# Two weight-row pairs of each gate/up column block as seven products of block sums

## The reference, cut to what matters

```python
D_FF = ((8 * D_MODEL + 3 * 256 - 1) // (3 * 256)) * 256     # 5632
h = _rmsnorm(x, ffn_norm[l])
gate, up = jnp.split(h @ w_gate_up[l], 2, axis=-1)
x = x + (jax.nn.silu(gate) * up) @ w_down[l]
```

## Time and profile before

| what | value |
|---|---|
| median of 3 runs | 2871.65 us (2871.58 to 2873.06) |
| span of the profiled execution | 2869.4 us |
| TensorE busy | 2863.4 us |
| VectorE busy | 1852.1 us |
| ScalarE busy | 1339.4 us |
| GpSimd busy | 868.4 us |

### The profile page before, as it was taken

How to read it: one execution, slowest core, us unless ns; L and a number is a source line. 1 busy time by engine, 2 the same in 40 slices (tenths; PEclk the granted TensorE clock), 3 DMA queues, 4 the chain that set the end, 5 groups by cost and what they waited for, 6 DMA issues and landing times.

```text
span 2869.4 us, 35463 instructions
## 1 busy us (share of the span) xinstructions
PE 2863.4 (100%) x12860; PEld 2372.1 (83%) x12860; DVE 1852.1 (65%) x2277; ACT 1339.4 (47%) x1564; POOL 868.4 (30%) x1477
## 2 busy tenths in 40 slices
PE   9999999999999999999999999999999999999999
PEld 8888888888888888888888888888888888888887
DVE  7599866687655555545575998666876555555554
ACT  5445554554544444444444455445545444444443
POOL 0055267355222322300000652773452313213000
PEclk9999999999999999999999999999999999999999
DMA  7666666776666666666666666667766666666554
GB/s 247 182 186 199 201 192 194 229 238 194 196 192 192 195 191 193 194 193 194 193 193 177 198 192 197 191 194 233 238 194 196 191 193 193 191 195 191 194 193 170
DMA packets 291296, 567.39 MB, mean 198 GB/s; under 512 B 18984, under 2 KB 24944, under 8 KB 291184
## 3 DMA queue, kind: packets, MB, share of 16 engines
q1 hardware_dynamic: 283888, 540.54, 61.8%
q10 hardware_dynamic: 7296, 25.44, 2.7%
HBM read 551.23 MB, written 14.68 MB: 197 GB/s over the span
## 4 chain that ended last, share of the span: by engine, by line
PE 98%; DVE 1%; ACT 0%; issue 0%; DMA 0%; DVEq 0%; ACTq 0%
PE acc L481 64%; PE acc L486 32%; PE acc L528 1%; DVE w_lo L1193 1%; PE acc L526 1%; PE acc L539 0%; DVE arena L1193 0%; DVE tmp L1193 0%; PE acc L519 0%; ACT w_hi L812 0%; PE acc L540 0%; DMA xs<-in_x_dram 0%; DVE arena L1211 0%; PE acc L498 0%; PE acc L654 0%
## 5 line engine op out<-in xcount | busy, mean ns | idle before, releaser
L1193 DVE TENSOR_TENSOR w_lo<-w_raw,w_hi 128x1024 fp32r<-128x1024 f32 x1024 | 1261.6, 1236 | 970.4 <-ACT w_hi L812 965.8
L812 ACT ACTIVATE w_hi<-w_raw 128x1024 fp32r<-128x1024 f32 x1024 | 1084.0, 1060 | 1461.4 <-PE acc L486 1414.6
L481 PE MATMUL acc<-w_hi,opa_hi 128*128 128x512 f32 (+1 forms) x2364 | 927.8, 392 | 0.6 <-ACT w_hi L812 0.6
L481 PE MATMUL acc<-w_hi,opa_lo 128*128 128x512 f32 (+1 forms) x2364 | 917.6, 388 | 0.0
L481 PE MATMUL acc<-w_hi,opb_hi 128*128 128x512 f32 x1728 | 672.9, 389 | 0.2
L481 PE MATMUL acc<-w_hi,opb_lo 128*128 128x512 f32 x1728 | 672.3, 389 | 0.0
L486 PE MATMUL acc<-w_lo,opa_hi 128*128 128x512 f32 (+1 forms) x2364 | 629.9, 388 | 0.1
L481 PEld LDWEIGHTS acc<-w_hi,opa_hi 128*128 128x128 f32 x2364 | 444.0, 188 | 94.4 <-issue 3.7
L486 PEld LDWEIGHTS acc<-w_lo,opa_hi 128*128 128x128 f32 x2364 | 442.7, 188 | 92.4 <-DVE w_lo L1193 2.0
L481 PEld LDWEIGHTS acc<-w_hi,opa_lo 128*128 128x128 f32 x2364 | 444.0, 188 | 88.2
L391 POOL COPY arena<-tmp 32x256 f32<-32x256 f32 x384 | 262.5, 684 | 732.3 <-DVE tmp L1211 717.3
(11 more groups left out here) (182 smaller groups left out, 1141.6 us busy)
## 6 DMA issues: line engine op xcount, KB each, us to landing
w_raw<-in_w_gate_up_dram SPq DMA_DIRECT2D x352, 512.0 KB, 4.4
w_raw<-in_w_in_dram SPq DMA_DIRECT2D x336, 512.0 KB, 3.6
w_raw<-in_w_down_dram SPq DMA_DIRECT2D x176, 512.0 KB, 4.6
w_raw<-in_w_branch_dram SPq DMA_DIRECT2D x64, 512.0 KB, 4.7
w_raw<-in_w_out_dram SPq DMA_DIRECT2D x64, 512.0 KB, 4.4
gate_store<-nat ACTq DMA_DIRECT2D x24, 512.0 KB, 3.9
arena<-gate_store ACTq DMA_DIRECT2D x24, 512.0 KB, 5.4
w_raw<-in_w_kv_b_dram SPq DMA_DIRECT2D x16, 512.0 KB, 4.3
```

Of the source, the lines that this page charges most:

```text
L481: pe.matmul(bank(pair, t, width), op[j][:, kt + k, t * P:(t + 1) * P], w_hi[:, s, k, 0:width], start=(first and k == 0 and j == 0), stop=F ...
L812: return act.activation(out, in_, ACT.Copy, scale=scale)
L1193: return dve.tensor_tensor(out, a, b, op)
```

## The change

In blocks 1 to 10 of each layer the units stand in another order (`FF_ORDER`; a pair is row block u and half h, 0 gate and 1 up). Two pairs of units, places 0 and 1 (row block pair 0, gate and up) and places 5 and 6 (row block pair 1), are multiplied together: with the two row tiles and the two `k` on the left, and `k` and gate/up on the right, each pair is a product of two matrices of 2 by 2 blocks. It goes by the seven products of the Strassen-Winograd form, each three matmuls, 21 in place of 24. Four left sums are made once per layer (`h_sums`). Three weight differences per pair are made by VectorE (`w_sums_12` changes the up unit's first row block in place; `w_sums_34`), rounded by ScalarE (`sums_hi`) and completed by VectorE (`w_sums_lo`). The products add up in banks 0, 1, 2 and in banks 4 to 7, which this stage did not use before; VectorE combines the latter (`parts`), adds them to the gate and up banks (`gate_sums`, `up_sums`) and then does what it did. TensorE has new waits: `w_sum_hi` and `w_sum_lo` for the sums, `part_emptied` for banks 4 to 7, and in the first pair's seventh product `dve_emptied` for bank 2. The core of the diff:

```diff
+FF_CLASSIC = [(u, h) for h in range(2) for u in range(UB)]
+FF_ORDER = [(0, 0), (0, 1), (2, 0), (3, 0), (4, 0), (1, 0), (1, 1), (5, 0), (6, 0), (7, 0)] + [(u, 1) for u in range(2, UB)]
+SEVEN = ((0, 1), (5, 6))
+FFU = 2 * UB
+assert all(FF_ORDER[a][0] == FF_ORDER[b][0] == i for i, (a, b) in enumerate(SEVEN)) and sorted(FF_ORDER) == sorted(FF_CLASSIC)
...
+                    for m, (u, h) in enumerate(FF_ORDER if c else FF_CLASSIC):
+                        unit(n, m, wgu, l, u, c * N + h * D_FF)
...
+                def product(b, op, at, w, start, stop, hi_need, lo_need):
+
+                    if hi_need:
+                        pe.wait_ge(*hi_need)
+                    for i in range(2):
+                        pe.matmul(acc[:, b, :], at(op[i]), w[0], start=(start and i == 0), stop=False)
+                    if lo_need:
+                        pe.wait_ge(*lo_need)
+                    return pe.matmul(acc[:, b, :], at(op[0]), w[1], start=False, stop=stop)
+
+                def seven(n, i, j):
+
+                    ma, mb = SEVEN[i]
+                    sa, sb_ = ma % RING, mb % RING
+                    first, last = i == 0, i == len(SEVEN) - 1
+                    k0 = KU * i
+                    made = sevens(l) * 2 + j * 4 + (2 * i - 4)
+
+                    def rows(k, t):
+                        return lambda op: op[:, k0 + k, t * P:(t + 1) * P]
+
+                    def summed(f):
+                        return lambda op: op[:, i, f]
+
+                    def unit_w(s, k):
+                        return w_hi[:, s, k], w_lo[:, s, k]
+
+                    def made_w(m):
+                        return [sum_w34[p][:, m] for p in range(2)]
+
+                    product(4, opb, rows(0, 0), unit_w(sa, 0), first, last, (hi_ready, n + (ma + 1)), (lo_ready, lo_count(n, ma)))
+                    product(0, opb, rows(1, 0), unit_w(sa, 1), first, False, None, None).then_inc(unit_done, 1)
+                    product(5, sum_op, summed(0), unit_w(sb_, 0), first, last, (hi_ready, n + (mb + 1)), (lo_ready, lo_count(n, mb)))
+                    product(6, sum_op, summed(1), sum_w2, first, last, (w_sum_hi, made + 1), (w_sum_lo, made + 1))
+                    product(7, sum_op, summed(2), made_w(0), first, last, (w_sum_hi, made + 2), (w_sum_lo, made + 2))
+                    product(1, opb, rows(1, 1), made_w(1), first, False, None, None).then_inc(w_sum_used, 1)
+                    if first:
+                        pe.wait_ge(dve_emptied, l * DVE_GROUPS + j * 2 + (CREDIT + V_FF))
+                    product(2, sum_op, summed(3), unit_w(sb_, 1), first, False, None, None).then_inc(unit_done, 1)
+
+                pe.wait_ge(h_sum_lo, l + 1)
                 with pe.Fori(1, NF) as j:
...
+                    pe.wait_ge(part_emptied, l * (NF - 1) + j)
+                    pe.wait_ge(dve_emptied, l * DVE_GROUPS + j * 2 + (CREDIT + V_FF - 1))
+                    for m, (u, h) in enumerate(FF_ORDER):
+                        if m in (SEVEN[0][0], SEVEN[1][0]):
+                            seven(n, SEVEN.index((m, m + 1)), j)
+                        elif m not in (SEVEN[0][1], SEVEN[1][1]):
+                            unit(n, m, opb, KU * u, h, (False, m == FF_ORDER.index((2, 1))), m in (9, FFU - 1))
...
+                def sums_hi(step3, step1):
+
+                    act.wait_ge(w_summed, step3 + 2)
+                    act.wait_ge(w_sum_used, step1 + 1)
+                    copy(sum_w2[0], w_sum[:, 0]).then_inc(w_sum_hi, 1)
+                    act.wait_ge(w_summed, step3 + 3)
+                    copy(sum_w34[0], w_sum[:, 1:3]).then_inc(w_sum_hi, 1)
+
+                def first_part(n, j):
+
+                    done(n, SEVEN[-1][1])
+                    act.wait_ge(dve_emptied, l * DVE_GROUPS + j * 2 + (CREDIT + V_FF))
+                    copy(cg[:, 0], acc[:, 4, :]).then_inc(first_out, 1)
...
+                def h_sums():
+
+                    base = l * 5
+                    a = [h_full[:, :, k, t * P:(t + 1) * P] for t in range(NT) for k in range(KU)]
+                    flat = [opb[p][:, 0:4].rearrange("p (a k) s -> p a k s", a=2).bitcast(F32) for p in range(2)]
+                    tt(h_full, flat[0], flat[1], ALU.add).then_inc(h_summed, 1)
+                    wait(h_summed, base + 1)
+                    tt(h_sum[:, :, 0], a[2], a[3], ALU.add).then_inc(h_summed, 1)
+                    tt(h_sum[:, :, 2], a[2], a[0], ALU.subtract).then_inc(h_summed, 1)
+                    wait(h_summed, base + 2)
+                    tt(h_sum[:, :, 1], h_sum[:, :, 0], a[0], ALU.subtract).then_inc(h_summed, 1)
+                    wait(h_summed, base + 4)
+                    tt(h_sum[:, :, 3], a[1], h_sum[:, :, 1], ALU.subtract).then_inc(h_summed, 1)
...
+                def w_sums_12(nq, ma, mb, step3):
+
+                    sa, sb_ = ma % RING, mb % RING
+                    wait(raw_landed[sa], nq + 16 * (ma // RING + 1))
+                    wait(raw_landed[sb_], nq + 16 * (mb // RING + 1))
+                    tt(raw[:, sb_, 0], raw[:, sb_, 0], raw[:, sa, 0], ALU.subtract).then_inc(w_summed, 1)
+                    wait(w_summed, step3 + 1)
+                    tt(w_sum[:, 0], raw[:, sb_, 1], raw[:, sb_, 0], ALU.subtract).then_inc(w_summed, 1)
+
+                def w_sums_34(ma, step3):
+
+                    wait(w_summed, step3 + 2)
+                    tt(w_sum[:, 1:3], raw[:, ma % RING], w_sum[:, 0].unsqueeze(1).to_broadcast([P, KU, N]),
+                       ALU.subtract).then_inc(w_summed, 1)
+
+                def w_sums_lo(step2):
+
+                    wait(w_sum_hi, step2 + 1)
+                    tt(sum_w2[1], w_sum[:, 0], sum_w2[0].bitcast(F32), ALU.subtract).then_inc(w_sum_lo, 1)
+                    wait(w_sum_hi, step2 + 2)
+                    tt(sum_w34[1], w_sum[:, 1:3], sum_w34[0].bitcast(F32), ALU.subtract).then_inc(w_sum_lo, 1)
+
+                def parts(j, n):
+
+                    wait(first_out, l * (NF - 1) + j)
+                    step(tt(part_sum, acc[:, 6, :], cg[:, 0], ALU.add))
+                    step(tt(cg[:, 1], acc[:, 7, :], part_sum, ALU.add), False)
+                    step(tt(nat[:, 0], acc[:, 5, :], part_sum, ALU.add), False)
+                    step(None)
+                    tt(nat[:, 1], acc[:, 5, :], cg[:, 1], ALU.add).then_inc(part_emptied, 1)
+
+                def gate_sums(j, n):
+
+                    wait(unit_done, n + (RING + 10))
+                    wait(part_emptied, l * (NF - 1) + j + 1)
+                    tt(cg, cg, bank(0), ALU.add).then_inc(dve_emptied, 1)
+
+                def gate_product(j):
+
+                    wait(dve_emptied, l * DVE_GROUPS + j * 2 + (CREDIT + V_FF + 1))
+                    wait(sig_ready, l * NF + j + 1)
+                    for t in range(NT):
+                        ins = dve.scalar_tensor_tensor(gg[:, t], cg[:, t], rx[:, 2 + t:3 + t], sg[:, t], ALU.mult, ALU.mult)
+                        step(ins, t == 1)
+
+                def up_sums(j, n):
+
+                    wait(unit_done, n + (RING + FFU))
+                    wait(part_emptied, l * (NF - 1) + j + 1)
+                    tt(nat[:, :, :], nat[:, :, :], bank(1), ALU.add).then_inc(dve_emptied, 1)
+                    wait(dve_emptied, l * DVE_GROUPS + j * 2 + (CREDIT + V_FF + 2))
+                    for t in range(NT):
+                        ins = dve.scalar_tensor_tensor(nat[:, t], nat[:, t], rx[:, 2 + t:3 + t], gg[:, t], ALU.mult, ALU.mult)
+                        step(ins, t == 1)
+                    wait(h_sb, l * NF + j + 1)
+                    turn(tmp[:, :], nat).then_inc(h_t, 1)
...
+                def ff_turn(j, n, nq, after, more):
+
+                    sb3, sa3 = sevens(l) * 3 + j * 6 - 3, sevens(l) * 3 + j * 6
+                    sb2, sa2 = sevens(l) * 2 + j * 4 - 2, sevens(l) * 2 + j * 4
+                    (a0, a1), (b0, b1) = SEVEN
+                    for m in range(FFU):
+                        at = m + RING
+                        if at == b0:
+                            w_sums_34(b0, sb3)
+                        if at == FFU + a0 and more:
+                            w_sums_34(a0, sa3)
+                        lo(n, at)
+                        if at == b0 - 1:
+                            w_sums_12(nq, b0, b1, sb3)
+                        if at == FFU + a0 - 1 and more:
+                            w_sums_12(nq, FFU + a0, FFU + a1, sa3)
+                        if at == b1:
+                            w_sums_lo(sb2)
+                        if at == FFU + a1 and more:
+                            w_sums_lo(sa2)
+                        if m == 7:
+                            parts(j, n)
+                        if m == 9:
+                            gate_sums(j, n)
+                        for f in after.get(m, ()):
+                            f()
+                        if m == 14:
+                            gate_product(j)
```

(48 more changed lines are left out.)

62 lines of the change are left out of this document (35 added, 27 removed).

## The result

| | before (four runs) | after (four runs) |
|---|---|---|
| median | 2871.61 us (2871.30 to 2873.06) | 2847.78 us (2847.15 to 2848.24) |
| span of the profiled execution | 2869.4 us | 2845.8 us |

The ratio is 0.9917 with an interval of 0.9905 to 0.9929: 23.8 us faster. The forecast was 2846.5.

What follows compares the result with a forecast made beforehand. TensorE, busy 2863.4 of 2869.4 us, was taken to bound the kernel. Median 2871.65 less 27.2 us for 120 removed products plus 2 us for the up bank gives 2846.5 us, range 2843.5 to 2861.

Steps and rivals of the forecast that it cites:

- The bound, the removed products, the step: TensorE alone sets the end; 120 products fewer at an unchanged 0.2267 us give 27.2 us, blocks of 42.16 us.
- Rival D: Products pay at issue on TensorE: a 0.11 us gap in each run of three, 31 us, so 2875; chance 0.11.
- rival E: TensorE's clock falls; the two groups' 42 products at 1.2 GHz would take double, 190 us more; chance 0.02.
- The sum: Median 2871.65 less 27.2 for the products plus 2 for the up bank gives 2846.5 us.
- The up bank: First group's seventh product waits for VectorE's up add; release wanted at 3.74, 0.1 us left; cost 0.1 a block, 2 in all.
- Rival B: Up bank waits visibly, VectorE's tail 0.3 to 1.0 us longer; at 0.6 a block, 2856.5 us; chance 0.26.
- The start of each layer: VectorE's five left sums and one remainder, at most 5.2 us a layer, are hidden by a remainder's 7.4 us slack.
- The load of unit 17: Differences for the next block's first group wait for it; lands at 32.8, VectorE comes at 33.7; landing free to 6.0 us.
- Rival C: Slower: VectorE stands at the load of unit 17; at 8.4 us landings, 2892 us; chance 0.06.
- The second group: At 12.92 us in the block; its last sum remainder at 14.2, needed at 16.1, spare 1.9 us.
- GpSimd: GpSimd was said to have the same work as before; busy 11.02 us a block.
- VectorE and ScalarE: VectorE rises from 23.4 to 37.7 us a block; ScalarE gets at most 5 us more and has 24 free.

Runs made afterwards that it cites:

- experiment 1: Changed kernel with the sixth product made twice, so each pair has eight products (24 matmuls) again; 2873.59 us, ratio 1.0007 to the kernel before.
- Experiment 7: Changed kernel with left sums made in block 0's second half and the first `part_emptied` credit raised by GpSimd; 2844.44 us, ratio 0.9906 to the kernel before.
- experiment 4: Changed kernel with each layer's left sums made in the second half of block 0 in place of the first; 2845.94 us.
- experiment 6: Changed kernel with the first credit for banks 4 to 7 (`part_emptied`) raised by GpSimd in place of VectorE; 2846.36 us.
- experiment 2: Changed kernel with the weight sums made once a layer and used for all blocks; 2847.78 us.
- experiment 3: Changed kernel with one unused 512-column addition on VectorE right ahead of the up sum; 2856.65 us, ratio 0.9948 to the kernel before.
- experiment 8: Changed kernel with GpSimd placing one piece of sixteen in the blocks behind the first; 2848.44 us.

## Why the prediction was right, step by step

**The bound, the removed products, the step.** Right. TensorE is full, the step stayed at 0.227 us in runs of three, and blocks take 42.16 us. Rival D (2875) falls by this and by experiment 1, rival E by the clock of 1.00 in every window.

**The sum.** Experiment 7 gives back 27.1 us. The changed kernel keeps 23.8, and the two parts that experiments 4 and 6 gain, 1.84 and 1.42, make up the rest: 27.1 - 3.3 = 23.8. The forecast took 27.2 - 2 = 25.2. The time came out 1.3 us above it. The 27.2 was right by its mechanism; that the rest came so close was luck, since the 2 us taken off for the up bank were not lost there, and the 3.3 us that were lost stood in two places at which the forecast had put nothing.

**The up bank.** The term of 0.1 us a block was mis-sized: it is 0 in 18 blocks. The lag it was drawn from was close. The sum ends 937.39 - 933.63 = 3.76 us into the block, forecast 3.66. The 0.10 stands ahead of the remainder: it starts 1.40 us into the block in place of 1.31, 0.12 behind the recorded end of the gate product (934.91), with a wait for VectorE's own result and two register steps between, where the forecast let it follow at once. By experiment 2 the floor of 3.66 itself was right. The room behind the sum is 0.13 us. The handoff was priced too dear: I wanted the release at 3.74, and by experiment 3 it may come at 3.76 + 0.13 = 3.89. So the two errors of this step, 0.10 and 0.15, went opposite ways. Rival B was right on the mechanism, as experiment 3 shows, and 0.13 us from beginning to cost time. The overlap of VectorE's operations, on which it hung, held: the sum starts at 936.18, 0.08 us before the recorded end of the remainder ahead of it.

**The start of each layer.** This step failed. "The slack of a remainder hides them" looked at VectorE's sums alone. ScalarE, in program order, waited 3.18 us for them with the sigmoids and three roundings behind, and by way of a late load TensorE paid at the up bank of the first changed block. The cost, 1.84 us for both layers, lies well under the 5.2 us a layer given as the price without cover. It was also the reason why TensorE waited at the seventh product in the first changed block, by 0.9 and 0.4 us, and in no later one.

**The load of unit 17.** Right in the steady blocks: VectorE comes to it 967.35 - 933.63 = 33.72 us into the block, forecast 33.7, and finds it landed. Rival C's mechanism came once a layer, ahead of the first changed block, from a late issue. (The free landing by the forecast's own figures is 33.7 + 0.55 - 28.4 = 5.85 us, not 6.0; nothing hung on it.)

**The second group.** "Spare 1.9 us" was too much. The last sum remainder ends at 946.76 + 2.21 = 948.97, 15.34 us into the block in place of 14.2. The 1.13 between are the slower operations there: 0.34 in the three differences, 0.40 in two remainders and 0.39 in the sums' remainders, against the same shapes later in the block or in experiment 8. About 0.8 us of spare was left, so it cost nothing.

**GpSimd.** "The same work" was right in count and wrong in time: 16.45 us a block for 11.02. I had looked for what its work needs and not for what VectorE's new work does to it.

**VectorE and ScalarE.** 37.97 us against 37.7 and 21.65 against 18.2 and at most 5 more (five operations of 1.04 us make 5.2), both as forecast; the weight sums cost 9.4 us a block by experiment 2, forecast 9.1.

**Not forecast**: the 1.5 us in the mixer, from one instruction more on VectorE. The sign named for a right forecast, waits in the seventh product alone and of a few tenths, did not hold by this and by the 0.9 us.

## What to carry to other kernels

Where one engine is full from end to end, taking work off it pays in full, so long as each added piece on the others meets its due time; price the pieces by due times and not by busy shares. Follow every added operation to all engines that wait for it in program order, the one that only rounds its result too, and look hardest at the first round of a loop, where the work of the start and that of the loop meet. When the steady part comes out exactly, the rest of the difference stands in the list of waits, one row for each cause; a row tells the place, and the cost can be larger (3.0 us listed for 8.9 us lost in experiment 3).

## What the runs showed of the hardware

**GpSimd and VectorE slow each other.** GpSimd's copies from `tmp` to `arena`, most of them for the down stage, min, median and max in ns over all 384, before and after:

```profile
L391 POOL COPY arena<-tmp x384: 390/396/1448, 498.3 to 2642.7; 32x256 f32<-32x256 f32 x192
```

```profile
L414 POOL COPY arena<-tmp x384: 390/1293/1449, 498.5 to 2620.4; 32x256 f32<-32x256 f32 x192
```

The copies are the same; what changed is that VectorE has less idle time between its operations, and now most of them take 1.3 us. Experiment 2 bears this out: with 9.4 us of VectorE's work gone they are back from 16.45 to 11.76 us a block. VectorE's side is the 0.88 for 0.69 us. The Trainium skill, page "SBUF — State Buffer", section "Who interferes with whom", says that a VectorE instruction with two SBUF inputs contends with a GpSimd instruction that reads SBUF, that one with at most one such input, outside the 2-port perf modes, doesn't, and that the port pair the two engines share is an exclusive lock. The trace agrees on the first two: remainders and differences are lengthened, while the two sums with a PSUM operand at 956.47 us take 1.41 beside the last of the copies, as they do in experiment 2 at 956.22, when the copies are done. GpSimd's side agrees too: the copy of 955.50 us, beside a remainder, takes 1.31, and the one of 956.85, beside these sums, 0.40. On the lock it agrees nearly. In experiment 8 the copy starts 0.14 us into a remainder that ends at 941.08, and ends 0.26 after that; the difference behind them ends 0.55 us after the copy, where a full hold would make it 0.69; the copy's 0.26 behind the remainder falls short of its 0.39 alone by as much.

**One instruction moves a wait.** A single semaphore raise at the start of VectorE's program delays one remainder by 0.36 us some 600 us later, and costs 1.5 us of time. Whether it is the place of the code behind it or something else was not tried. So a difference of 1.5 us between two versions of this kernel says nothing on the edit itself until the waits are compared.
